# A third place in the ring of projection weights, sixteen small zero matmuls, and one count for four conditional loads

## The reference

```python
# layers 0 and 1
h = rms_norm(x, norm1_g) * (1 + sc1) + sh1          # sc, sh, g from c_act @ w_ada + b_ada
q, k, v, cb, cc, ch, su, sv = split(h @ w_in)
merged = concat(rms_norm(attention(q, k, v)), rms_norm(conv(cb, cc, ch)), rms_norm(sgu(su, sv)))
x = x + g1 * (merged @ w_out)
h2 = rms_norm(x, norm2_g) * (1 + sc2) + sh2
x = x + g2 * peer_ffn(h2)       # 8 heads x 16 experts per token, two gathered rows of 1024 each

# layer 2 (gated linear attention) and layer 3 (a linear recurrence)
x = x + g1 * mixer(h)           # h @ w_in, chunks or a scan, @ w_out
# 16 experts, each token takes 2 of one group of 4
for e in range(16):
    he = silu(t @ w_gate[e]) * (t @ w_up[e])
    out = out + combine[:, e:e+1] * (he @ w_down[e])
```

## Time and profile before

| what | value |
|---|---|
| median of three runs | 2777.35 us |
| the profiled execution's own time | 2791.36 us |
| its span, first to last instruction | 2789.6 us |
| mean granted clock of PE | 0.928 of 2.4 GHz |
| busy: PE, DVE, ACT, POOL | 2356.4, 1232.2, 662.4, 657.1 us |
| moved by DMA | 934.35 MB |

### The profile page before, as it was taken

One profiled execution on the slowest core, in us unless ns is written; L12 is line 12 of the kernel. 1 busy time (PEld: TensorE's weight loads), 2 busy tenths in 40 slices (PEclk: granted clock), 3 DMA queues, 4 the chain that ended last, 5 costly groups with the idle time before them and its releaser, 6 DMA issues.

```text
span 2789.6 us, 25669 instructions
## 1 busy us (share of the span) xinstructions
PE 2356.4 (84%) x9276; PEld 1240.1 (44%) x9276; DVE 1232.2 (44%) x2873; ACT 662.4 (24%) x1860; POOL 657.1 (24%) x831
## 2 busy tenths in 40 slices
PE   7899877778788989977877787987998989789988
PEld 3676433333333577433333333446443456644433
DVE  1336666776664325667667755553200022330001
ACT  1213232333233122333223333111111123111111
POOL 1103333333332102433433332101222000122200
PEclk9999999998889989999999989987999999899999
DMA  9749999999997647999999997863799235669980
GB/s 366 305 151 365 422 421 421 421 421 421 421 422 315 273 196 316 386 421 421 421 422 421 421 421 329 329 263 136 324 421 421 115 121 213 254 280 421 421 339 16
DMA packets 130127, 934.35 MB, mean 335 GB/s; under 512 B 14289, under 2 KB 16337, under 8 KB 16593
## 3 DMA queue, kind: packets, MB, share of 16 engines
q0 software_dynamic: 114768, 835.96, 72.5%
q1 hardware_dynamic: 15232, 96.75, 9.0%
HBM read 1070.02 MB, written 1.05 MB: 384 GB/s over the span
## 4 chain that ended last, share of the span: by engine, by line
PE 47%; DMA 31%; DVE 16%; ACT 4%; issue 2%; SPq 0%; DVEq 0%; POOL 0%; ACTq 0%; POOLq 0%
PE units L738 12%; PE units L1222 12%; PE accs L992 11%; DMA arena<-rows,idx 11%; DMA wide<-rows,idx 8%; DMA wide<-experts 5%; DMA ring<-stream 4%; DVE wide L1974 3%; DVE arena L1974 2%; PE units L753 2%; DMA arena<-experts 2%; PE units L1187 2%; PE accs L1270 2%; ACT arena L1461 1%; PE accs L821 1%
## 5 line engine op out<-in xcount | busy, mean ns | idle before, releaser
L992 PE MATMUL accs<-wide,arena 128*128 128x512 f32 x1040 | 515.8, 651 | 147.0 <-ACT arena L1461 146.8
L992 PE MATMUL accs<-arena 128*128 128x512 f32 x1008 | 481.4, 632 | 96.5 <-ACT arena L1461 96.3
L992 PEld LDWEIGHTS accs<-wide,arena 128*128 128x128 f32 x1040 | 211.2, 208 | 437.7 <-issue 250.4
L1222 PE MATMUL units<-wide,arena 128*64 128x512 f32 (+1 forms) x1728 | 372.4, 601 | 26.2 <-DMA wide<-experts 21.2
L647 POOL DMA_INDIRECT wide<-rows,idx x260 | 245.7, 945 | 607.7 <-PE accs L992 419.6
L992 PEld LDWEIGHTS accs<-arena 128*128 128x128 f32 x1008 | 201.9, 203 | 371.1 <-issue 247.4
L647 POOL DMA_INDIRECT arena<-rows,idx x252 | 238.3, 946 | 361.7 <-PE accs L992 325.4
L738 PE MATMUL units<-arena,ring 128*128 128x256 f32 (+1 forms) x1344 | 300.4, 386 | 27.3 <-ACT arena L1351 14.0
L1324 ACT ACTIVATE arena<-units 128x512 f32<-128x512 f32 (+1 forms) x186 | 106.5, 575 | 841.5 <-PE units L738 300.8
L738 PEld LDWEIGHTS units<-arena,ring 128*128 128x128 f32 x1344 | 256.8, 200 | 72.4 <-issue 36.6
L1222 PE MATMUL units<-arena 128*64 128x512 f32 (+1 forms) x960 | 235.4, 594 | 17.1 <-DMA arena<-experts 10.9
(11 more groups left out here) (317 smaller groups left out, 2158.3 us busy)
## 6 DMA issues: line engine op xcount, KB each, us to landing
wide<-experts POOLq DMA_DIRECT2D x123, 1024.0 KB, 18.4
wide<-experts SPq DMA_DIRECT2D x93, 1024.0 KB
wide<-ada POOLq DMA_DIRECT2D x88, 1024.0 KB, 10.2
arena<-experts POOLq DMA_DIRECT2D x69, 1024.0 KB, 20.3
ring<-stream SPq DMA_DIRECT2D x62, 1024.0 KB, 6.5
arena<-experts SPq DMA_DIRECT2D x51, 1024.0 KB
arena<-side SPq DMA_DIRECT2D x8, 1024.0 KB, 8.3
wide<-ada SPq DMA_DIRECT2D x7, 1024.0 KB, 13.4
```

The lines of the kernel that those rows point to most:

```text
L992: ins = mm(o[:, half * 512:(half + 1) * 512], diag[:, i % (2 * GROUP), :], row_slot(PICKS * l + i)[:, D + half * 512:D + (half + 1) * 512] ...
L1222: ins = mm(o[j * n:(j + 1) * n, :], act[:, j * n:(j + 1) * n], exp_slot(l, i)[:, c * 512:(c + 1) * 512], start=start, stop=stop, skip_grou ...
```

## The change

Three edits. `RING` goes from 2 to 3, so that `ring` is 24 KB a partition in place of 16, and a slot's load waits for the slot three before it. The zero operand shrinks from 512 to 128 columns, and the banks are opened by 16 matmuls of 128 columns. The conditional loads of one step (four lanes) count on one of four semaphores in turn, in place of eleven semaphores by place, and PE waits once for a step.

```diff
-RING = 2
+RING = 3
...
+def extra_step(l, i):
+    return ((l - DEPTH) * EXTRA + i - OWN) // 4
...
-        zeros = sb("zeros", [P, 512], BF16)
+        zeros = sb("zeros", [P, P], BF16)
...
-        extra_landed = [sem(f"extra_landed{i}") for i in range(NE)]
+        extra_landed = [sem(f"extra_landed{i}") for i in range(4)]
...
-                                :, bass.ds(e, 1), s, :], cond=used).then_inc(extra_landed[exp_at(l, i)], 16)
+                                :, bass.ds(e, 1), s, :], cond=used).then_inc(
+                                    extra_landed[extra_step(l, i) % 4], 16)
...
-                    for i in loads:
-                        sems = exp_landed if i < OWN else extra_landed
-                        pe.wait_ge(sems[exp_at(l, i)], 16 * landings_to(l, i, i >= OWN))
+                    if loads[0] >= OWN:
+                        n = extra_step(l, loads[0])
+                        pe.wait_ge(extra_landed[n % 4], 16 * 4 * (n // 4 + 1))
+                    else:
+                        for i in loads:
+                            pe.wait_ge(exp_landed[exp_at(l, i)], 16 * landings_to(l, i))
...
-                for b in range(4):
-                    mm(acc[b][:, :], zeros[:, 0:P], zeros[:, :], start=True, stop=False, skip_group_check=True)
+                for b in range(16):
+                    mm(accs[:, b * P:(b + 1) * P], zeros[:, :], zeros[:, :], start=True, stop=False,
+                       skip_group_check=True)
```

More of the change, by code:

```diff
@@ L309, in uses_before, with landings_to @@
     return m // NE
-def landings_to(l, i, extra):
+def landings_to(l, i):
     at = ((l - DEPTH) * LOADS + i) % NE
-    return sum(1 for n in range((l - DEPTH) * LOADS + i + 1) if n % NE == at and (n % LOADS >= OWN) == extra)
+    return sum(1 for n in range((l - DEPTH) * LOADS + i + 1) if n % NE == at and n % LOADS < OWN)
+def extra_step(l, i):
+    return ((l - DEPTH) * EXTRA + i - OWN) // 4
 def program(nc, x, w, side, experts, ada, small, first_const, gla_const, keys, rows, out):
```

## The result

| | before | after |
|---|---|---|
| median (4 runs each) | 2779.6 us | 2743.57 us |
| lowest to highest | 2768.8 to 2788.65 | 2740.02 to 2747.13 |
| profiled execution | 2791.36 | 2747.13 |
| span | 2789.6 | 2745.4 |
| mean granted clock | 0.928 | 0.932 |

The ratio of the changed kernel to the one before is 0.987, 95% interval 0.9851 to 0.9889. The forecast was 2747 us, and 1.1% less; it became 1.3% less.

A forecast was written before the change was run, and what follows sets the result against it. Bytes bound the long stages; in the projection stretches PE sets the pace and waits for ring loads. 2791.36 - 24.2 - 6.8 + 0.9 = 2761.3 us profiled, 2747 us as median (2777.35 - 30.1), range 2737 to 2768.

The forecast's parts named there:

- The waits, -24.2: Four projection stretches: PE's 14 waits for ring loads, 24.2 us in all, should all go with the third place.
- What passes the gain on: Stages after the projections: gathers and later work move up whole, long stages keep their length; cost 0.
- The third sum in layer 2: Layer 2: would end at 1833 against PE's need at 1844, leaving 11 us of room.
- The clock, -6.8: Four projection slots behind ring waits: 7.1 us instead of 8.8 at full clock, 1.7 us each, 6.8 in all.
- The price of the zeros, +0.9: Bank openings, twice in the program: sixteen 128-column matmuls for four of 512 cost 0 to +1.7 us, taken as +0.9.
- The grouped count, 0: Lane tiles: fewer waits a step change nothing, as the queue takes them ahead of the matmuls; 0 us.
- The clock stays: Projection slots: all ring waits go but the four slow slots stay at 0.81; -23.3 us, 2754 us, chance 0.18.
- Only defers: Projection stretches: loads issued together share bandwidth, waits return a slot later; half the waits go, -11.2, 2766 us, chance 0.17.
- The bytes decide: Full stages: earlier ring loads push back ada, row and expert loads; six boundaries of 2.5 us, 2794 us, chance 0.05.

## Why the prediction was right, point by point

**The waits, -24.2.** Right. All 14 are gone in three profiles of the changed kernel. Four profiles with the loads as late as before have 24.2, 25.7, 22.2 and 25.2 us in all, 24.3 in the mean.

**What passes the gain on.** Right. The means of three profiles of the changed kernel against four with late loads (before twice, the other edits alone, three places late), by the start of each norm's matmuls:

| stretch | late loads | early loads | less | forecast | waits in the late ones | slots, less |
|---|---|---|---|---|---|---|
| layer 0 to the second norm | 180.5 | 173.0 | 7.5 | 7.8 | 4.5 | 1.5 |
| layer 0 gathers | 694.1 | 695.7 | -1.6 | 0 | 0 | -0.4 |
| layer 1 to the second norm | 156.7 | 151.8 | 4.9 | 4.4 | 2.9 | 1.7 |
| layer 1 gathers | 692.2 | 692.8 | -0.6 | 0 | 0 | -0.1 |
| layer 2 to the second norm | 192.6 | 178.0 | 14.6 | 10.9 | 10.4 | 4.4 |
| layer 2 tiles, layer 3 to the second norm | 495.5 | 485.5 | 10.0 | 7.0 | 6.6 | 3.2 |
| layer 3 tiles and end | 366.4 | 365.2 | 1.2 | 0 | 0 | 0 |

(The forecast is the waits of the earlier trace rows and 1.7 us for the one slow slot of each, with the 0.9 for the zeros in the sixth row, though the second opening of the banks lies in the seventh. The last two columns are means too: PE's waits for the ring with late loads, and by how much less time PE was busy with the projection slots with early ones.) The stretches without ring loads are the same within 2 us, and in the others waits and slots add up to what was measured within 1.5 us. The third sum in layer 2, which I had given 11 us of room, caused no wait.

**The clock, -6.8.** The term that was mis-sized, and reasoned too simply. I counted the four slots that one profile had at the low clock behind a ring wait. Over all projection slots PE was busy for 466.1 us in the mean of the four profiles with late loads and for 455.7 in the three with early ones: the term measured 10.4 us, not 6.8. The slots behind a ring wait aren't slow in the same places each time (in layer 2 three slots took 22.6 us in the second profile of before and 20.87 in the first), so four from one profile was too low a count. Waits and slots make 34.7 of the 36.1 us by which the profiles' mean spans differ (2778.0 and 2741.9; 36.0 by medians, 30.1 forecast). Near as the total came, it is the sum of waits that were right, a clock term too small by 3.6 us and zeros too dear by 0.8. What the count can't tell apart is how much of the 10.4 us is the pause and how much chance of the few profiles. The profiled pair differs by 44 us, of which 4.9 are the PV matmuls of layer 0 and more of the same kind is likely.

The Trainium skill ("TensorE: Matmul & The Clock Gate", section "HAM oscillation — how this bites in real kernels") says that pauses for a DMA between groups of matmuls send the array back to half clock and cost a second time on top of the pause. The trace agrees that the slot behind the pause is slow, 8.8 us against 7.1. It doesn't agree that this always costs: the run with filled waits has the four slots at full clock and the same time, ratio 0.9995.

**The price of the zeros, +0.9.** Too high: 0.92 against 0.89 us each, 0.1 in all. The figures that the prediction took from the Trainium skill ("TensorE: Matmul & The Clock Gate", section "Wait — 56ns, not 53.3ns?"), 0.89 against 0.86 as an estimate, were the better ones; the f32 transposes that I took as the upper end were no likeness for bf16 matmuls.

**The grouped count, 0.** Right, by the run of the two edits alone, and a lane tile's six steps read 20.81 and 20.74 us in the changed kernel, as 20.74 before. What I hadn't seen is that these two edits pay with room and semaphores, which the third place needs.

**Rivals.** "The clock stays" is out by the windows of the result. "Only defers" is out: loads of 10.6 us in a stretch at 420 GB/s, longer than before, and no wait. Whether ring loads slow each other isn't shown: the two took 1.1 to 1.2 us longer than the two of the earlier trace rows, but they were issued at 2351.3 and 2359.9 and so were out together for 2 us only, and in the other two profiles of the changed kernel such loads took 9.1 to 10.3 us. The second landed at 2370.5, 2.6 us before the last slot began, so the run of four slots is over before the lead is used up. "The bytes decide" is out: no wait for expert loads came up in the projection stretches and those for ada pieces are 12.1 us in all against 12.0, and the stages at 406 to 417 GB/s kept their length.

## What to carry to other kernels

Where a ring feeds an engine, compare the load's time from issue to landing in the fullest stretch (here 9.4 to 10.6 us) with the work that lies between the release of a place and the need of its data (here one slot, 7.1 us): the median load (6.5 us) fitted and the loads that mattered didn't. One more place was worth those differences, 24.3 us, and 10 more by faster slots, and it is worth looking for a kilobyte in an operand that needs less and for semaphores that can be shared to pay for it. Don't add the loss by clock to a wait before asking whether the next load is hidden by it: with the loads still late, four slots at full clock in place of the low one changed the time by less than 0.2%.

## What the runs showed of the hardware that I hadn't expected

- Useless matmuls in a pause pay on top of the third place: with the softmax and norm pauses filled, the kernel is 8.6 us faster than the changed kernel, and its six runs spread over 1.8 us where those of the changed kernel spread over 12.3 and those of before over 24.8. That much of what looks like noise of this kernel is the level of TensorE's clock behind pauses of 3.5 to 5.3 us fits this; it wasn't shown run by run.
- The same 48 matmuls take 5.47 us or 10.34, in layer 0 or in layer 1, from one execution of the same program to the next.
- Sixteen bf16 matmuls of 128 columns take 0.92 us, four of 512 columns 0.89: the sixteen weight loads, 98 ns each, lie beside the matmuls and cost next to nothing.
